# Query slabs of one projection over 512 token columns instead of 768, and shift columns stored twice

## What is computed

```python
def odd_mixer(h, hc, w_in, w_out, sink, rows, cols, with_ctx):
    def project(t):
        p = t @ w_in
        q, k, v = jnp.split(p, [C_WIDTH, C_WIDTH + C_KV_WIDTH], axis=-1)
        return split_heads(q, C_Q_HEADS), split_heads(k, C_KV_HEADS), split_heads(v, C_KV_HEADS)
    q, k, v = project(h)
    qc, kc, vc = project(hc)
    q = axial_rope(q, rows, cols)
    k = axial_rope(k, rows, cols)
    y = window_gqa_blocks(q, k, v, kc, vc, sink) @ w_out
    yc = None
    if with_ctx:                      # False in this layer
        yc = ctx_attention(qc, kc, vc, sink) @ w_out
    return y, yc
```

## Time and profile before

| | |
|---|---|
| median of 3 runs | 3478.97 us |
| lowest, highest | 3462.59, 3479.81 us |
| profiled execution, its own time | 3482.57 us |
| its span in the trace | 3480.7 us |
| TensorE busy | 3168.8 us (91%) |
| VectorE, ScalarE, GpSimd busy | 1733.0, 1099.9, 1055.6 us |
| mean granted TensorE clock | 0.937 of full |

### The profile page before, as it was taken

The page is one execution under the profiler, slowest core; times in us unless marked ns, Lnnn a source line. Parts: engine busy times, 40 slices in busy tenths (PEclk is TensorE's granted clock), DMA queues, the critical chain, the costliest instruction groups (busy, mean ns, idle before and its releaser), DMA issues.

```text
span 3480.7 us, 49444 instructions
## 1 busy us (share of the span) xinstructions
PE 3168.8 (91%) x16984; PEld 2523.9 (73%) x16984; DVE 1733.0 (50%) x2913; ACT 1099.9 (32%) x1911; POOL 1055.6 (30%) x579
## 2 busy tenths in 40 slices
PE   6778699999989898899987988899999999899997
PEld 3656578888877666889965844677787866678876
DVE  4665777854336664524344636442433247733423
ACT  3144142111122364522242113452223216643222
POOL 1121122323223212344423401144444411244443
PEclk9889899999999999999998968799999979999998
DMA  6101323433111001222221200122233200022222
GB/s 238 68 1 43 111 85 133 167 121 121 59 56 43 19 1 49 73 91 90 92 65 48 97 15 1 53 95 92 89 101 94 71 31 2 13 87 94 94 93 79
DMA packets 74340, 258.77 MB, mean 74 GB/s; under 512 B 9456, under 2 KB 12016, under 8 KB 72688
## 3 DMA queue, kind: packets, MB, share of 16 engines
q1 hardware_dynamic: 60256, 205.61, 17.7%
q10 hardware_dynamic: 13968, 51.65, 4.4%
HBM read 253.03 MB, written 2.10 MB: 73 GB/s over the span
## 4 chain that ended last, share of the span: by engine, by line
PE 82%; DVE 6%; issue 6%; ACT 3%; DVEq 1%; DMA 1%; SPq 1%; POOL 1%; ACTq 0%; POOLq 0%; PEldq 0%
PE ps L805 56%; PE ps L783 6%; PE ps L2404 2%; PE ps L2418 2%; PE ps L2597 1%; PE ps L418 1%; PE ps L1466 1%; PE ps L1659 1%; DVE ps L381 1%; PE ps L2661 1%; PE ps L1471 1%; PE ps L2559 1%; ACT w_hi L625 1%; PE ps L2558 1%; PE ps L1078 1%
## 5 line engine op out<-in xcount | busy, mean ns | idle before, releaser
L743 POOL TENSOR_TENSOR w_lo<-w_raw,w_hi 128x1024 fp32r<-128x1024 f32 (+1 forms) x373 | 918.2, 2464 | 1766.1 <-ACT w_hi L625 1766.1
L625 ACT ACTIVATE w_hi<-w_raw 128x1024 fp32r<-128x1024 f32 (+1 forms) x373 | 385.7, 1038 | 1237.4 <-PE ps L805 1013.9
L805 PE MATMUL ps<-h_hi,w_hi 128*128 128x258 f32 (+2 forms) x1824 | 325.2, 332 | 48.7 <-ACT w_hi L625 44.5
L805 PEld LDWEIGHTS ps<-h_hi,w_hi 128*128 128x128 f32 x1824 | 273.5, 195 | 87.7 <-issue 46.2
L805 PE MATMUL ps<-h_hi,w_lo 128*128 128x258 f32 (+2 forms) x1824 | 308.4, 321 | 0.0
L805 PE MATMUL ps<-h_lo,w_hi 128*128 128x258 f32 (+2 forms) x1824 | 307.5, 321 | 0.0
L805 PEld LDWEIGHTS ps<-h_hi,w_lo 128*128 128x128 f32 x1824 | 265.3, 190 | 27.6
L805 PEld LDWEIGHTS ps<-h_lo,w_hi 128*128 128x128 f32 x1824 | 264.0, 189 | 26.9
L805 PE MATMUL ps<-hb_hi,w_hi 128*128 128x512 f32 x672 | 171.0, 396 | 1.9 <-issue 1.8
L901 DVE CAST act_hi<-f_t 128x512 f32 (+1 forms) x88 | 164.0, 1863 | 12.6
L805 PE MATMUL ps<-hb_hi,w_lo 128*128 128x512 f32 x672 | 169.8, 394 | 0.0
(11 more groups left out here) (342 smaller groups left out, 5308.7 us busy)
## 6 DMA issues: line engine op xcount, KB each, us to landing
w_raw<-in_ffn_in SPq DMA_DIRECT2D x176, 512.0 KB, 3.2
mod_row<-in_w_mod_rows ACTq DMA_DIRECT2D x80, 512.0 KB, 4.4
w_raw<-in_ffn_out SPq DMA_DIRECT2D x64, 512.0 KB, 3.3
w_raw<-in_ev_in SPq DMA_DIRECT2D x26, 512.0 KB, 3.2
w_raw<-in_ffn_out SPq DMA_DIRECT2D x32, 384.0 KB, 3.0
w_raw<-in_od_in SPq DMA_DIRECT2D x21, 512.0 KB, 3.3
mod_ring<-in_w_mod SPq DMA_DIRECT2D x8, 1024.0 KB, 13.0
w_raw<-in_wo_in SPq DMA_DIRECT2D x12, 512.0 KB, 3.3
```

Source lines behind the costliest of these rows:

```text
L625: act.activation(k.w_hi[:, s, 0:self.KT * P], k.w_raw[:, s, 0:self.KT * P], ACT.Copy).then_inc(k.sems["w_hi_ready"], 1)
L743: ins = pool.tensor_tensor(k.w_lo[:, s, 0:self.KT * P], k.w_raw[:, s, 0:self.KT * P], k.w_hi[:, s, 0:self.KT * P].bitcast(F32), ALU.subtract)
L805: ins = pe.matmul(k.ps[:, 2 * s + g, 0:t1 - t0], w[:, s, c * P:(c + 1) * P], h[:, c, t0:t1], start=(n == 0), stop=(n == len(parts) - 1))
```

## The change

`Pre` and `Gate` get a flag `twice`, set for `wo_in` alone. With it the two shift columns are written at 512 and 513 and again at 770 and 771, and the context tokens move to columns 514 to 769. `Linear` gets `latent=range(2, 10)`, the query slabs: these use the groups 0 to 255 and 256 to 513, and their eviction touches tokens 0 to 511 alone. The other four slabs take 0 to 511 and 514 to 771. The tiles `h_hi` and `h_lo` grow by two columns, which moves what lies behind them by 128 bytes; `lam_p`, a small tile used later, shares its place with another to make room.

```diff
@@ Pre
+        self.shift_at = (SEQ, TOK + 2) if twice else (self.T,)
     def act_shift(self, act, chain):
-            chain.link(act.activation(self.hi[:, :, self.T:self.T + 2], src if n == 2 else src.to_broadcast([P, DC, 2]), ACT.Copy))
+            for at in self.shift_at:
+                ins = act.activation(self.hi[:, :, at:at + 2], src if n == 2 else src.to_broadcast([P, DC, 2]), ACT.Copy)
+            chain.link(ins)
     def dve_shift(self, dve):
...
+            for at in self.shift_at:
+                dve.tensor_tensor(self.lo[:, :, at:at + 2], src if n == 2 else src.to_broadcast([P, DC, 2]), self.hi[:, :, at:at + 2].bitcast(F32), ALU.subtract)
+    def columns(self, t0, t1):
+        return slice(t0 + 2, t1 + 2) if self.twice and t0 >= SEQ else slice(t0, t1)
     def act_hi(self, act, c, m=None):
-            ins = act.activation(self.hi[:, at, t0:t1], k.x[:, at, t0:t1], ...)
+            ins = act.activation(self.hi[:, at, self.columns(t0, t1)], k.x[:, at, t0:t1], ...)
@@ Linear
-        self.groups = [(0, SEQ // 2), (SEQ // 2, SEQ + 2)] if self.halves else [(0, SEQ), (SEQ, TOK + 2)] if self.shifted else groups
+        self.groups = [(0, SEQ // 2), (SEQ // 2, SEQ + 2)] if self.halves else ([(0, SEQ), (SEQ + 2, TOK + 4)] if norm.twice else [(0, SEQ), (SEQ, TOK + 2)]) if self.shifted else groups
+    def columns(self, m):
+        return [(0, SEQ // 2), (SEQ // 2, SEQ + 2)] if m in self.latent else self.groups
@@ Linear.empty
+        tokens = self.tokens
         if self.norm:
             r = k.n_r[:, :T].unsqueeze(1)
+            if self.latent and m in self.latent:
+                tokens, two = X_ONLY, lambda ap: ap.rearrange("p (a b) -> p a b", a=2)
+                dst, src, r = dst[:, :, 0:SEQ], k.ps[:, 2 * s:2 * s + 2, 0:SEQ // 2], two(k.n_r[:, 0:SEQ])
...
-            ins = eng.scalar_tensor_tensor(dst, src, scale, r, ALU.mult, ALU.mult)
+            ins = eng.scalar_tensor_tensor(two(dst[:, 0, :]) if tokens is not self.tokens else dst, src, scale, r, ALU.mult, ALU.mult)
...
-                for j, (t0, t1) in enumerate(self.tokens):
+                for j, (t0, t1) in enumerate(tokens):
@@ Linear.tensor, tile
-                for g, (t0, t1) in enumerate(self.groups):
+                for g, (t0, t1) in enumerate(self.columns(m) if self.latent else self.groups):
@@ plan
-    g = Gate(k, X_CTX, k.gate_ffn[:, 0], k.scale_mix[:, 1], k.shift_mix[:, 1], k.h_hi, k.h_lo)
-    wo_in = Linear(k, d["wo_in"], ..., norm=g.pre, tiles=WO_TILES)
+    g = Gate(k, X_CTX, k.gate_ffn[:, 0], k.scale_mix[:, 1], k.shift_mix[:, 1], k.h_hi, k.h_lo, twice=True)
+    wo_in = Linear(k, d["wo_in"], ..., norm=g.pre, tiles=WO_TILES, latent=range(2, 10))
```

More of the change, by code:

```diff
@@ L180, with __init__ @@
 class Pre:
-    def __init__(self, kit, cols, shift, groups, hi, lo):
-        self.kit, self.cols, self.shift, self.groups, self.hi, self.lo = kit, cols, shift, groups, hi, lo
+    def __init__(self, kit, cols, shift, groups, hi, lo, twice=False):
+        self.kit, self.cols, self.shift, self.groups, self.hi, self.lo, self.twice = kit, cols, shift, groups, hi, lo, twice
         self.T = groups[-1][1]
+        self.shift_at = (SEQ, TOK + 2) if twice else (self.T,)
         self.b = {n: kit.reserve(n, c) for n, c in (("pre_hi", DC), ("pre_lo", DC), ("mean_ready", 1), ("r_ready", 1))}
@@ L192, in act_shift @@
             src = self.shift.rearrange("p j c -> p c j")
-            chain.link(act.activation(self.hi[:, :, self.T:self.T + 2], src if n == 2 else src.to_broadcast([P, DC, 2]), ACT.Copy))
+            for at in self.shift_at:
+                ins = act.activation(self.hi[:, :, at:at + 2], src if n == 2 else src.to_broadcast([P, DC, 2]), ACT.Copy)
+            chain.link(ins)
     def dve_shift(self, dve):
         if self.shift is not None:
-            n, at = self.shift.shape[1], slice(self.T, self.T + 2)
+            n = self.shift.shape[1]
             src = self.shift.rearrange("p j c -> p c j")
             dve.wait_ge(self.kit.sems["pre_hi"], self.b["pre_hi"] + 1)
-            dve.tensor_tensor(self.lo[:, :, at], src if n == 2 else src.to_broadcast([P, DC, 2]), self.hi[:, :, at].bitcast(F32), ALU.subtract)
+            for at in self.shift_at:
+                dve.tensor_tensor(self.lo[:, :, at:at + 2], src if n == 2 else src.to_broadcast([P, DC, 2]), self.hi[:, :, at:at + 2].bitcast(F32), ALU.subtract)
+    def columns(self, t0, t1):
+        return slice(t0 + 2, t1 + 2) if self.twice and t0 >= SEQ else slice(t0, t1)
     def act_hi(self, act, c, m=None):
@@ L205, in act_hi @@
         for j, (t0, t1) in enumerate(self.groups):
-            ins = act.activation(self.hi[:, at, t0:t1], k.x[:, at, t0:t1], ACT.Identity, bias=0.0, scale=self.cols[:, j, at])
+            ins = act.activation(self.hi[:, at, self.columns(t0, t1)], k.x[:, at, t0:t1], ACT.Identity, bias=0.0, scale=self.cols[:, j, at])
         ins.then_inc(k.sems["pre_hi"], 1)
@@ L213, in dve_lo @@
         for j, (t0, t1) in enumerate(self.groups):
-            ins = dve.scalar_tensor_tensor(self.lo[:, at, t0:t1], k.x[:, at, t0:t1], self.cols[:, j, at], self.hi[:, at, t0:t1].bitcast(F32), ALU.mult, ALU.subtract)
+            ins = dve.scalar_tensor_tensor(self.lo[:, at, self.columns(t0, t1)], k.x[:, at, t0:t1], self.cols[:, j, at], self.hi[:, at, self.columns(t0, t1)].bitcast(F32), ALU.mult, ALU.subtract)
         ins.then_inc(k.sems["pre_lo"], 1)
@@ L428, with __init__ @@
 class Gate(Stage):
-    def __init__(self, kit, groups, cols, norm_cols, shift, hi, lo):
+    def __init__(self, kit, groups, cols, norm_cols, shift, hi, lo, twice=False):
         super().__init__(kit)
@@ L436, in __init__ @@
         self.b = {n: kit.reserve(n, c) for n, c in (("y_mean", 1), ("y_rstd", 1), ("gate_t", DC), ("gate_x", DC), ("sq_ready", DC), ("sq_used", DC - 1))}
-        self.pre = Pre(kit, norm_cols, shift, groups, hi, lo)
+        self.pre = Pre(kit, norm_cols, shift, groups, hi, lo, twice)
     def tensor(self, pe):
@@ L515, with __init__ @@
 class Linear(Stage):
-    def __init__(self, kit, w, hi, lo, groups, mode, dst=None, segs=None, side=None, rows=None, norm=None, post=None, tiles=None):
+    def __init__(self, kit, w, hi, lo, groups, mode, dst=None, segs=None, side=None, rows=None, norm=None, post=None, tiles=None, latent=()):
         super().__init__(kit)
         self.rows, self.norm, self.post = rows, norm, post
-        self.order, self.beside = tiles, None
+        self.order, self.beside, self.latent = tiles, None, latent
         self.side, self.feeds = side, False
@@ L2206, in memory @@
 def memory(kit):
-    H, A, Y, TMP, W, C = 24576, 73856, 123008, 147584, 159872, 184448
+    H, A, Y, TMP, W, C = 24576, 73984, 123136, 147712, 160000, 184576
     k, at = kit, kit.at
     k.x = at("x", [P, DC, TOK], F32, 0)
-    k.h_hi = at("h_hi", [P, DC, TOK + 2], F32R, H)
-    k.h_lo = at("h_lo", [P, DC, TOK + 2], F32R, H + 24640)
+    k.h_hi = at("h_hi", [P, DC, TOK + 4], F32R, H)
+    k.h_lo = at("h_lo", [P, DC, TOK + 4], F32R, H + 24704)
     k.ha = (at("ha_hi", [P, DC, SEQ], F32R, H), at("ha_lo", [P, DC, SEQ], F32R, H + 16384))
@@ L2318, in memory @@
     k.lam = small("lam", [P, 4, HD])
-    k.lam_p = small("lam_p", [P, 2, HD])
     k.lam_s = small("lam_s", [P, 8])
@@ L2336, in memory @@
     k.w2 = small("w2", [P, 2, HD])
+    k.lam_p = at("lam_p", [P, 2, HD], F32, c[0])
     k.gel = small("gel", [P, 4, 32])
@@ L2484, in plan @@
                         ("out", 1): (88, 8, 1, (0,), [(1, "gate_ffn", (0,))])})
-    g = Gate(k, X_CTX, k.gate_ffn[:, 0], k.scale_mix[:, 1], k.shift_mix[:, 1], k.h_hi, k.h_lo)
-    wo_in = Linear(k, d["wo_in"], k.h_hi, k.h_lo, X_CTX, "copy", k.qkv, [(0, 2, HD ** -0.5), (2, 12, 1.0)], norm=g.pre, tiles=WO_TILES)
+    g = Gate(k, X_CTX, k.gate_ffn[:, 0], k.scale_mix[:, 1], k.shift_mix[:, 1], k.h_hi, k.h_lo, twice=True)
+    wo_in = Linear(k, d["wo_in"], k.h_hi, k.h_lo, X_CTX, "copy", k.qkv, [(0, 2, HD ** -0.5), (2, 12, 1.0)], norm=g.pre, tiles=WO_TILES, latent=range(2, 10))
     WindowBeside(k, wo_in, k.rot_a[:], k.table[:, 0], k.rot_c1,
```

## The result

The changed kernel takes 3434.86 us (median of 4 executions, 3420.69 to 3439.55) against 3476.22 us beside it: a ratio of 0.9888, 95% interval [0.9861, 0.9915]. So it is faster by about 1.1%, some 39 us, where 0.62% was forecast and 3439 us was the lower end of the range.

The account below looks back on a forecast made before the run. TensorE was taken to bound wo_in's query slabs; 19.0 us from seven slabs at full clock plus 2.7 us from the first made 21.7 us, from the median 3478.97 to 3457 us (0.62% less), range 3439 to 3471 us.

Parts of the forecast that it names:

- the part that was costed: TensorE in the eight query slabs of wo_in: fewer columns per matmul pair gain 21.7 us in all.
- the narrow slab: Query slabs of wo_in: 48 matmuls go from 8.49 to 5.77 us, 2.72 us less per slab.
- slab 2: First query slab, begun at half clock: 9.86 us becomes 7.1 us, 2.7 us less.
- two cases for VectorE: Query slabs: L647 finishes before GpSimd's L743, L1108 ending about 3.3 us earlier, or is held, 0.6 us earlier.
- The second pair of shift columns: One more ScalarE instruction (0.21 us) and VectorE instruction (0.18 us), taken as 0; 0.4 us in all without cover.
- The step that failed: Context columns two further on and tiles moved by 128 bytes change no count or shape: 0 ± 0.5 us.
- Rival 2: Later stretches: the clock's return gives more (3435 to 3447 us, chance 0.14) or takes part (3463 to 3475 us, 0.14).
- Rival 1: Written-out query slabs: weight loads set a 7.80 us floor per slab, losing 12.4 us, 3467 us; chance 0.08.
- The estimate of 98 ns: Spacing of a 256-column matmul by the skill's rule: saves 6 us, giving 3473 us; chance 0.02 of a rival's 0.08.
- Rivals 3 and 4: 3: stage from 2080 us stays at half clock, ending slower, chance 0.04. 4: change doesn't take effect, no separate chance.

Follow-up runs that it names:

- e12_all_but_narrow: Kernel before with the changed kernel's full memory map, every slab's columns as before: 3458.21 us, ratio 0.9957, 26.6 us less at equal clock.
- e8_weights_only: Kernel before with only w_hi and w_lo, and the constants behind them, moved by 128 bytes: 3477.19 us, ratio 0.9988.
- e3_all128: Kernel before with h_hi, h_lo and all behind them moved 128 bytes together, x staying: 3472.42 us, ratio 0.9995.

## Why the prediction was wrong

*The mechanism of the part that was costed was right.* TensorE was the wait in the query slabs and stayed it; the forecast from the feed-forward's rows gave the narrow slab within 0.08 us (5.77, measured 5.69 to 5.70) and slab 2 within 0.03 us (7.1, measured 7.13). Of its two cases for VectorE, between which it did not choose, the one with L647 ahead of GpSimd came true. The second pair of shift columns was to cost nothing: the first sum of squares in the chain went from 1.38 to 1.52 us and all other pieces there stayed, so 0.1 us.

*The step that failed* is the sentence "Context columns that stand two further on, and tiles moved by 128 bytes, change no count and no shape; I bound them at 0 ± 0.5 us." Measured by e12_all_but_narrow, the moved tiles alone are worth 26.6 ± 0.8 us, more than the part that I costed. With some 20 us from the narrow slabs and some 5 us lost through the clock (below) that makes the 41 us between the medians (3476.22 and 3434.86). Counts and shapes did stay; the time of a matmul does not follow from them alone. By slabs: 88 x 0.113 = 9.9 us in the second block's feed-forward, 26 x 0.13 to 0.16 = 3.9 in its first in-projection, 21 x 0.10 = 2.1 in its third, some 2.3 in its two out-projections, and 9 in the first block, where the stride of `h_hi` and `h_lo` counts too: 27 us.

The sign could be read in the trace of before, had I looked beyond the stage of the change. Hb slabs took 5.553 us and act slabs 5.440 with the same 24 matmuls of 512 columns at the same clock, and within the hb slab the three products took 1.86, 1.83 and 1.86 us.

*Rival 2*, more gained through the clock, gave the interval (3435 to 3447 us) at whose edge the result fell (3434.86 us, and 3437.12 in the repetition), for the wrong reason; coming that close was luck. In the profiled pair the stretch near 2050 us was indeed 17 us shorter at half clock, about 5 us of the 50.9. But over all executions the changed kernel spent 437 us at half clock and before 419, which costs it some 5 us. The price that rivals 2 and 3 put on such time, half of it, was too high as well: between executions it is 0.300 us per us. Rival 1, a floor by weight loads, did not show: a written-out slab with its rotation took 6.55 us, less than the 7.80 us of weight loads in the earlier trace rows. The estimate of 98 ns for a matmul of 256 columns, made from the Trainium skill, TensorE: Matmul & The Clock Gate, section "Back-to-back issue gap", is contradicted by 5.70 us / 48 = 119 ns, and its slope, 33 ns for 256 columns, by 2.69 us / 24 = 112 ns. Rivals 3 and 4 did not occur.

## What to carry to other kernels

Compare the time of groups that have equal shapes, clock and count all over the kernel before costing an edit: where they differ, something else than the work sets them, and an edit that moves tiles can change it. In a kernel whose matmuls stand back to back with a weight load each, try the memory map by itself, with the moving tile and the weights starting a multiple of 256 bytes apart, and let a control that moves both together stand beside it. Where totals scatter with the clock, count slabs, or compare executions at equal time at half clock.

## What was not expected of the hardware

A stream of 128x512 matmuls, each with its own 128x128 fp32r weight load, is spaced at 5.440 / 24 = 227 ns when moving tile and weights stand a multiple of 256 bytes apart, at 229 ns when they are 192 off, and at 232 to 233 ns when 128 or 160 off. The last costs some 6 ns per matmul, 2.4 to 2.9%. Moving the weights (and the constants behind them) is enough to change it (e8_weights_only), and moving all tiles but `x` together changes nothing (e3_all128). The Trainium skill, TensorE: Matmul & The Clock Gate, section "Step-by-step: what each phase is for", says that the moving operand and the weight load have SBUF read ports of their own, so that loading the next weights takes no bandwidth from the running matmul. Here the spacing does depend on where the weights lie relative to the moving operand, 227 to 233 ns, for which that statement leaves no room. That the two reads disturb each other, in a bank of the memory or elsewhere, would explain it; no run shows it.

The shift addition and GpSimd's subtraction show who comes first: begun within 0.01 us of each other, VectorE's two took 2.97 us; begun 0.28 us ahead, the remaining one took 0.49 and GpSimd's went from 2.41 to 2.47. The Trainium skill, SBUF — State Buffer, section "Who interferes with whom", has it that when VectorE runs in a 2-port mode, which `tensor_scalar` can enter, whichever of the two is issued first holds the shared ports for its whole instruction and the other is blocked. The trace agrees as far as VectorE goes: in the earlier trace rows its two end 0.55 us after GpSimd's. For GpSimd it shows little: VectorE had 0.21 us left to run, and GpSimd's instruction became 0.06 us longer; and a lead of 0.01 us in the trace did not put VectorE first.
